# Second halves of the expert weight units through GpSimd's DMA queue, first halves through SyncE's

## The reference, cut to what matters

```python
for e in range(N_EXPERTS):                       # 8
    y = y + combine[..., e:e + 1] * _swiglu(h, exp_gate[e], exp_up[e], exp_down[e])
# _swiglu(h, g, u, d) = (silu(h @ g) * (h @ u)) @ d ;  D_MODEL = 1024, D_FF_EXPERT = 2816
```

## Time and profile before

| what | us |
|---|---|
| median of 3 runs | 1901.89 (1899.53 to 1903.06) |
| the profiled execution | 1902.75 |
| its span, first to last instruction | 1900.6 |

### The profile page before, as it was taken

How to read it: one execution, slowest core, us unless ns; L and a number is a source line. 1 busy time by engine, 2 the same in 40 slices (tenths; PEclk the granted TensorE clock), 3 DMA queues, 4 the chain that set the end, 5 groups by cost and what they waited for, 6 DMA issues and landing times.

```text
span 1900.6 us, 21384 instructions
## 1 busy us (share of the span) xinstructions
PE 1742.4 (92%) x8068; PEld 1433.9 (75%) x8068; DVE 1297.6 (68%) x1583; ACT 998.4 (53%) x1341; POOL 68.7 (4%) x78
## 2 busy tenths in 40 slices
PE   6899978899899968998799898999999999999994
PEld 4777767688778758987687676888888878888782
DVE  5574456745454365766454546999999989898897
ACT  5753263343333342434343334777777777777671
POOL 1004100100000000000000000000000000000001
PEclk8999989899999989999799998999999999999997
DMA  9552253344433424555155445999999999999892
GB/s 316 181 185 79 67 166 117 100 133 155 154 129 127 131 91 155 178 179 186 50 177 180 130 156 169 368 328 369 338 353 349 340 354 340 355 333 370 284 375 103
DMA packets 198462, 410.93 MB, mean 216 GB/s; under 512 B 12879, under 2 KB 46266, under 8 KB 198330
## 3 DMA queue, kind: packets, MB, share of 16 engines
q1 hardware_dynamic: 195050, 398.20, 60.8%
q0 software_dynamic: 3280, 11.02, 1.9%
HBM read 407.19 MB, written 1.98 MB: 215 GB/s over the span
## 4 chain that ended last, share of the span: by engine, by line
PE 79%; DVE 10%; ACT 4%; DMA 4%; issue 3%; POOL 1%; PEldq 0%; SPq 0%; DVEq 0%; ACTq 0%; PEld 0%; POOLq 0%
PE ps L508 23%; PE ps L510 22%; PE ps L509 22%; DVE w_lo L431 3%; PE ps L1320 2%; ACT w_hi L425 2%; PE ps L1139 1%; PE ps L1293 1%; DMA raw<-in_exp_up 1%; PE ps L677 1%; PE ps L678 1%; ACT hf L1430 1%; DMA raw<-in_w_mod 1%; DMA raw<-in_exp_gate 1%; PE ps L705 1%
## 5 line engine op out<-in xcount | busy, mean ns | idle before, releaser
L431 DVE TENSOR_TENSOR w_lo<-raw,w_hi 128x1024 fp32r<-128x1024 f32 (+1 forms) x760 | 892.6, 1216 | 230.4 <-ACT w_hi L425 218.8
L425 ACT CAST w_hi<-raw 128x1024 fp32r<-128x1024 f32 (+1 forms) x760 | 763.9, 1047 | 413.9 <-PE ps L510 342.7
L508 PE MATMUL ps<-w_hi,gT_hi 128*128 128x512 f32 x792 | 315.8, 399 | 2.8 <-issue 2.8
L510 PE MATMUL ps<-w_hi,gT_lo 128*128 128x512 f32 x792 | 310.6, 392 | 0.0
L509 PE MATMUL ps<-w_lo,gT_hi 128*128 128x512 f32 x792 | 310.4, 392 | 0.0
L508 PE MATMUL ps<-w_hi,prodT_hi 128*128 128x512 f32 x528 | 212.3, 402 | 8.8 <-DVE prod_dense L2143 5.2
L510 PE MATMUL ps<-w_hi,prodT_lo 128*128 128x512 f32 x528 | 208.2, 394 | 0.0
L509 PE MATMUL ps<-w_lo,prodT_hi 128*128 128x512 f32 x528 | 207.8, 394 | 0.0
L508 PEld LDWEIGHTS ps<-w_hi,gT_hi 128*128 128x128 f32 x792 | 149.7, 189 | 33.5 <-issue 3.9
L510 PEld LDWEIGHTS ps<-w_hi,gT_lo 128*128 128x128 f32 x792 | 149.8, 189 | 32.3
L509 PEld LDWEIGHTS ps<-w_lo,gT_hi 128*128 128x128 f32 x792 | 150.0, 189 | 29.7
(11 more groups left out here) (358 smaller groups left out, 2015.0 us busy)
## 6 DMA issues: line engine op xcount, KB each, us to landing
raw<-in_exp_gate SPq DMA_DIRECT2D x176, 512.0 KB, 5.3
raw<-in_exp_up SPq DMA_DIRECT2D x176, 512.0 KB, 5.2
raw<-in_exp_down SPq DMA_DIRECT2D x176, 512.0 KB, 5.4
raw<-in_w_mod SPq DMA_DIRECT2D x96, 512.0 KB, 4.6
raw<-in_w_in_conv SPq DMA_DIRECT2D x24, 512.0 KB, 6.2
raw<-in_ffn_gate SPq DMA_DIRECT2D x22, 512.0 KB, 4.6
raw<-in_ffn_up SPq DMA_DIRECT2D x22, 512.0 KB, 5.0
raw<-in_ffn_down SPq DMA_DIRECT2D x22, 512.0 KB, 4.2
```

Source lines behind the costliest of these rows:

```text
L425: nc.scalar.copy(w_hi[:, s, cols], raw[:, n % RAW, cols]).then_inc(sem("w_hi_ready"), 1)
L431: nc.vector.tensor_tensor(w_lo[:, s, cols], raw[:, n % RAW, cols], w_hi[:, s, cols].bitcast(F32), ALU.subtract).then_inc(sem("w_ready"), 1)
L508: nc.tensor.matmul(out, a[0], b[0], start=start, stop=False)
L510: return nc.tensor.matmul(out, a[1], b[0], start=False, stop=stop)
```

## The change

The three units that the first expert starts with are loaded as before. Of every other expert unit, 8 x 33 - 3 = 261 of them, SyncE issues part 0 only, and GpSimd issues part 1, with the same wait on `w_ready`, from a loop over all experts that stands in its program ahead of the wait for `gathers_done`. These second halves signal semaphores of their own (`raw_second{slot}`), and ScalarE waits for those. Sizes, buffers, and the work of the other engines stay the same.

```diff
@@ act_split
             for part, cols in enumerate(unit_parts(n)):
-                act.wait_ge(sem(f"raw_landed{n % RAW}_{part}"), val(16 * (n // RAW + 1), 16 * FFN_UNITS // RAW, e))
+                if part == 1 and e is not None and (e or n >= U_MOE + RAW):
+                    act.wait_ge(sem(f"raw_second{n % RAW}"), 16 * (e * (FFN_UNITS // RAW) + (n - U_MOE) // RAW))
+                else:
+                    act.wait_ge(sem(f"raw_landed{n % RAW}_{part}"), val(16 * (n // RAW + 1), 16 * FFN_UNITS // RAW, e))
@@ the helper, moved out of the SyncE program
+        def load(eng, n, e=None, halves=(0, 1)):
+            for (nk, src), (part, cols) in zip(weight_unit(t, n, e), enumerate(unit_parts(n))):
+                if part not in halves:
+                    continue
+                if n >= RAW:
+                    parts = part + 1 if cols.stop <= unit_parts(n - RAW)[part].stop else 2
+                    eng.wait_ge(sem("w_ready"), val(2 * (n - RAW) + parts, 2 * FFN_UNITS, e))
+                dst = raw[:, n % RAW, cols].rearrange("p (k n) -> p k n", k=nk)
+                landed = f"raw_landed{n % RAW}_{part}" if len(halves) == 2 or part == 0 else f"raw_second{n % RAW}"
+                eng.dma_start(dst, src).then_inc(sem(landed), 16)
@@ SyncE
             for e in range(N_EXP):
                 for u in range(FFN_UNITS):
-                    load(U_MOE + u, e)
+                    load(sp, U_MOE + u, e, (0, 1) if e == 0 and u < RAW else (0,))
@@ GpSimd, loop over the four layer norms
                 elif k == 3:
+                    for e in range(N_EXP):
+                        for u in range(FFN_UNITS):
+                            if e or u >= RAW:
+                                load(pool, U_MOE + u, e, (1,))
                     pool.wait_ge(sem("gathers_done"), 1)
```

More of the change, by code:

```diff
@@ L545, in _ @@
             sp.dma_start(const[:, :], t["const"]).then_inc(sem("const_in"), 16)
-            load(0)
+            load(sp, 0)
             rows(R_QG, 3, 0, t["q_a_gain"].rearrange("b (r n) -> (b r) n", n=P))
@@ L553, in _ @@
             for n in range(1, U_MOE):
-                load(n)
+                load(sp, n)
             for e in range(N_EXP):
                 for u in range(FFN_UNITS):
-                    load(U_MOE + u, e)
+                    load(sp, U_MOE + u, e, (0, 1) if e == 0 and u < RAW else (0,))
             for i in range(TILES):
```

## The result

The changed kernel takes 1928.02 us (median of 4 runs, 1924.35 to 1932.58) against 1900.71 for the kernel before (1898.97 to 1903.06): 1.0144 times the time before, 95% interval 1.0118 to 1.0171, some 27 us more. The forecast was 1902, and the range ended at 1918. The profiled execution took 1932.58 us.

The account below looks back on a forecast made before the run. TensorE was taken to set the pace in the experts, with DMA 2% quicker. Terms 0 + 0 + 0 + 0 on a profiled 1902.75 us, which lies 0.86 above the median, gave about 1902 us; 8-in-10 range 1898 to 1918.

Parts of the forecast that it names:

- latency of the new path: Step on the raw-buffer loop in the experts: GpSimd's issue adds 0.36 us, shrinking queueing gives it back, cost 0.
- 17 units: Units of each one-tile expert, about 17, where the prediction saw landings already waited for and lateness would bite.
- Second halves late: Rival: GpSimd's halves land late where landings are already waited for in the experts; +15 us, 1917 us, chance 0.24.
- deciding point: Issue-to-landing time of GpSimd's halves, some 6.3 us, from which late second halves would decide the outcome.
- Dearer bytes: Rival: GpSimd's bytes cost more DMA engine time in the experts, 2.83 against 2.72 us a unit; about +5, 1907 us, chance 0.14.
- the 13% of the earlier trace: Extra span per MB of queue 0's packets over queue 1's, 0.172% against 0.153, in the kernel before.
- rate with two queues, no loss: Step on expert weight loads: two queues move data no slower than SyncE's alone, 402 against 383 GB/s; no gain, no loss.
- GpSimd beside VectorE: Step: GpSimd's issues leave `w_lo` subtractions unchanged; cost 0 to 0.5 us on a few halves, inside the cushion.
- two-port lock: Skill's warning that VectorE's two-port modes block GpSimd's descriptors; 2.5 us more per half, loop of 10.6 us; not adopted.
- The moved queues: Step: `last_rows` loads behind GpSimd's 261 waits, and SP's final stores, lose nothing; cost 0.
- The removed issues: Step: 261 SP issues of 0.37 us, some 95 us, are off the path; gain 0.
- holes vanish: Rival: TensorE's hole at the last expert's start and a little in the first expert go; -5, 1897 us, chance 0.10.

Follow-up runs that it names:

- relay of second halves: Kernel before, all halves on SyncE's queue, but each second half waits for a one-column GpSimd multiplication before SyncE issues it; 1.0130, 1922.18 us.
- light kernel with GpSimd's queue: Kernel before with three quarters of each expert half loaded and second halves on GpSimd's queue; 0.9988, 1897.79 us.
- experts in turn: Kernel before with odd experts' halves all on GpSimd's queue, even experts' all on SyncE's; 1.0034, 1905.60 us.
- SyncE, one release more: Kernel before, SyncE's queue only, each second half waiting for one more half's release by VectorE before its issue; 1.0088, 1921.95 us.
- Units in turn: Kernel before with both halves of odd units on GpSimd's queue, of even units on SyncE's; 1.0182, 1934.53 us.
- with empty instructions: Kernel before with twelve no-operations on SyncE ahead of each second half's issue, which delayed nothing; 1.0019, 1905.39 us.
- both halves relayed: Kernel before, SyncE issuing every half, each only after its own one-column GpSimd multiplication following the release; 1.0132, 1928.00 us.
- light, SyncE alone: Kernel before with three quarters of each expert half loaded, all on SyncE's queue; 0.9976, 1899.63 us.

## Why the prediction was wrong

**The step that failed** is the latency of the new path: "with SP's 5.8 plus 0.36, 6.2 us, the queueing shrinks by what the issue grows, and nothing is lost [...] I take the first". It is wrong twice. The size: the difference between the queues is 0.62 us, because GpSimd also starts 0.30 us after a release where SyncE starts after 0.03; the step counted from the issue's start on. The rule: it let queueing give back the whole lateness. The relay of second halves has SyncE's single queue, and its late halves landed as long after their issue as before (5.6 us against 5.5); it cost 1.3%. The light kernel with GpSimd's queue keeps the lateness and the two queues, takes the shortage away, and costs nothing.

The step also counted six halves in flight, where the mean was 3.6 (391 halves of 5.46 us in 591 us). With a loop of 8.07 us against 8.16 the spare was 0.09, as the prediction itself worked out, in a tight stretch; over the six experts the median landing was 5.4 us and one in ten took 6.4 or more, so that it is the spread that eats the spare. Had the step kept 5.8 and added 0.27 and 0.35, an estimate made afterwards, it would have had 8.07 + 0.62 = 8.69 us, 2.90 a unit against 2.72, and over the 17 units of each expert where landings are waited for 0.18 x 17 x 7 = 21 us. Measured: 27. The 17 units are the prediction's, and the two halves of a unit are not both late, so the nearness is in part luck.

**Second halves late** was the rival that came nearest, with its sign and place right and its sizes wrong. It gave +15 us and a deciding point of some 6.3 us from GpSimd's issue to landing. Medians were 5.5 to 5.8 us, under that point, and the loss was there: the tail and the start of the issue are not in a median from issue to landing. Of the signs that the prediction named for this rival three held: the DMA share fell, ScalarE's landing waits more than doubled, and TensorE waits for `w_lo`. The fourth, that lateness raises GpSimd's landings alone, did not. SyncE's medians over the whole execution hide it (5.1 to 5.5 us, 5.2 to 5.4 before); in the experts the longest of SyncE's first halves went from 7.0 to 9.2 us, more than GpSimd's 8.1. So late halves are not the whole account.

**Dearer bytes** fell. Queue 0 now took 22.3 / 147.88 = 0.151% of the span per MB, queue 1 39.9 / 261.34 = 0.153; the 13% of the earlier trace rows belonged to other loads. The step "rate with two queues, no loss" is not borne out: the rate fell from 348 to 332 GB/s, and not because fewer halves were on their way, with 375 halves of 5.88 us in 591 us, 3.7 in the mean, against 3.6. But two queues aren't needed for that either: the relay of second halves, on one queue, moved 339 GB/s. "DMA: Bandwidth & Descriptors" of the Trainium skill, section "Issuing engines are not separate DMA queues", says that transfers of every issuer run on the same 16 engines and interleave. The trace agrees: halves of the two queues land together, as at 1203.6 and 1203.7 us, which halves of one queue never did here.

**GpSimd beside VectorE**: right that nothing happens to the subtractions, 1223 ns against 1225, and issues of 704 to 751 ns (1225 to 1245 us). The two-port lock that the prediction quoted from the Trainium skill did not come about beside them, as the prediction had read from the `w_lo` rows. (Its loop of 10.6 us would be 3.5 us a unit against 2.72, 30% more and not a fifth.)

**The moved queues** cost nothing: of the rest of GpSimd's program, the `last_rows` loads waited for TensorE as before (changed kernel, from 1860 us, by line):

```profile
L588 POOL DMA_DIRECT2D last_rows<-in_ln_g x1 | 0.5, 528 | 7.4 <-PEq L1399 7.4
```

**The removed issues** brought nothing, as forecast, and the rival *holes vanish* fell for this kernel: the first expert took 265.9 us against 265.0. (With all halves on GpSimd's queue, with experts in turn, and in the light kernel with GpSimd it took 258.6 to 258.7 us; no run here shows why.) The hole at the last expert's start comes later in the changed kernel, between 1795 and 1805 us, and is still there on VectorE, now behind a late copy (4.49 us before):

```profile
1802.07 2.36 DVE L434 TENSOR_TENSOR w_lo<-raw,w_hi 128x1024 fp32r<-128x1024 f32 x2 [3.29 <-ACT w_hi L428]
```

**What stays open.** The cost doesn't grow simply with the lateness. With second halves alone late by 0.34 us (relay, median) it is 1.3%, by 0.62 (the change) 1.4%; with both late by 0.62 (GpSimd alone) 0.7%; with both by 0.82 in the mean 1.3%; with 1.6 and 0.44 us (SyncE, one release more) 0.9%. Units in turn cost 1.8%. Part of the disorder is the first expert, which took 258.6 to 273.4 us for reasons that no run shows.

The next table leaves it out: from the start of expert 1 to the last subtraction of expert 7, in the one profiled execution of each kernel (two of the same kernel can differ by 4 to 5 us, as the changed one's do), worked out from the starts of `w_lo`. Beside it stands how many halves, from 1178 to 1769 us, landed within 0.7 us of the one before.

| kernel | queues at once | experts 1 to 7, us | landed within 0.7 us |
|---|---|---|---|
| before; with empty instructions | 1 | 719.7; 719.8 | 0%; 0% |
| experts in turn | 1, but for the borders | 724.4 | 0% |
| all on GpSimd | 1 | 730.0 | 0% |
| second halves relayed | 1 | 738.8 | 0% |
| second halves wait for one release more | 1 | 740.1 | 0% |
| both halves relayed | 1 | 751.9 | 0% |
| all on ScalarE | 1 | 748.7 | 0% |
| second halves of down units on GpSimd | 2 | 728.7 | 3% |
| second halves on ScalarE | 2 | 731.5 | 5% |
| first halves on GpSimd | 2 | 737.3 | 7% |
| units in turn | 2 | 742.6 | 6% |
| second halves of gate and up units on GpSimd | 2 | 744.1 | 4% |
| the change; once more | 2 | 746.9; 751.4 | 9%; 9% |
| light, SyncE alone | 1 | 715.2 | 0% |
| light, second halves on GpSimd | 2 | 713.7 | 6% |

Two queues leave a mark that one never does: some halves land in pairs. On one queue the shortest distance between two landings is 0.89 us in the light kernel and at least 1.11 in the others. That a half which is needed first is held up by the other queue's, as in the stall above, is the reading nearest to it. What that costs is not separated from the lateness: with lateness alone the relay of second halves lost 19 us in these experts, and the relay of both 32; the change lost 27 and 32. What the change lost beyond the first relay, 8 to 13 us, may be the second queue or the greater lateness. It also seems that lateness that differs inside a pair costs more than the same lateness for both halves (19 us at 0.34, against 10 at 0.62), but no run isolates that. What is shown is that lateness on one queue is enough for a loss of this size (some two thirds of it with second halves alone late, all of it with both), and that with time to spare there is no loss.

## What to carry to other kernels

Before a DMA is moved to another issuer, work out the loop of its buffer from release to release, with the issuer's wake-up and its whole issue, and compare it with the time in which the consumer comes round; if nothing is to spare, each tenth of a microsecond of lateness may be paid for, even where DMA engines and consumer both look full. A queue's typical landing time says little: look at the longest, on every queue, and at who waits; a half on the queue that was not touched can be the one that comes last. Here SyncE's 95 us of issues were never waited for, so that there was nothing to win.

## What the runs showed of the hardware

- GpSimd started its issue 0.30 us after VectorE's release, SyncE 0.03 us; the issue of a 512 KB load took GpSimd 0.72 us with 2 KB rows and 0.53 with 4 KB rows, SyncE 0.37 and 0.33.
- A GpSimd multiplication of one column took 0.20 us in a gap between VectorE's subtractions, and three in a row 2.83 beside them, while GpSimd's DMA issues kept their length beside the same subtractions.
- Halves on one queue, whoever issued them, landed in order and never less than 0.89 us apart (median distance 1.35 us before); with two queues 3 to 9% of them landed within 0.7 us, and the longest landing of SyncE's own first halves went from 7.0 to 9.2 us.
- With three quarters of the bytes TensorE was busy 591.00 of 591 us and the kernel gained 0.2%: the experts were at TensorE's pace already, and no version here with all its bytes beats the kernel before.
